# Cache pages in units of two pages of one cache, 8 KB on each partition

## The reference

```python
# 8 sequences, 16 pages of 128 tokens each, 8 stick-breaking and 8 forgetting heads of 128
gather = lambda cache: cache[page_table].reshape(B, past, *cache.shape[2:])
# stick breaking: A[t,s] = sigmoid(z_ts) * prod_{s<j<t} (1 - sigmoid(z_tj))
z = jnp.einsum('bqhd,bkhd->bhqk', q, k) * SCALE
later = lax.cumsum(log_stay, axis=3, reverse=True) - log_stay
a = jnp.exp(jax.nn.log_sigmoid(z) + later)
# forgetting: softmax with logit[t,s] += c[t] - c[s], c = cumsum(log f)
```

## Time and profile before

| | us |
|---|---|
| median of three runs | 1514.88 |
| the profiled execution | 1516.05 |
| its span, first to last instruction | 1514.3 |
| TensorE, VectorE busy | 1315.7, 673.4 |
| granted TensorE clock, mean | 0.939 |

### The profile page before, as it was taken

The page is one execution under the profiler, slowest core; times in us unless marked ns, Lnnn a source line. Parts: engine busy times, 40 slices in busy tenths (PEclk is TensorE's granted clock), DMA queues, the critical chain, the costliest instruction groups (busy, mean ns, idle before and its releaser), DMA issues. The chain is left out here.

```text
span 1514.3 us, 26133 instructions
## 1 busy us (share of the span) xinstructions
PE 1315.7 (87%) x8622; PEld 870.3 (57%) x8622; DVE 673.4 (44%) x4778; ACT 233.6 (15%) x453; POOL 75.4 (5%) x119
## 2 busy tenths in 40 slices
PE   7999788889789899856899987789999999999992
PEld 4678455566556566533667743466666565655561
DVE  4437855676676675677846466021000100000004
ACT  2111002112212212213011021101111010111011
POOL 1000000000000000001000001001100010001000
PEclk8899989899999999976999998979999999999997
DMA  9776999999999999999999989999999999999984
GB/s 302 248 260 229 385 397 391 396 383 381 382 377 390 383 379 392 387 405 398 351 403 402 401 320 390 399 414 379 422 428 428 427 424 423 422 419 414 416 341 178
DMA packets 170382, 570.39 MB, mean 377 GB/s; under 512 B 17401, under 2 KB 75562, under 8 KB 156954
## 3 DMA queue, kind: packets, MB, share of 16 engines
q1 hardware_dynamic: 145616, 541.70, 91.4%
q10 hardware_dynamic: 21762, 22.58, 4.3%
q0 software_dynamic: 2896, 4.86, 0.9%
HBM read 558.26 MB, written 15.67 MB: 379 GB/s over the span
## 5 line engine op out<-in xcount | busy, mean ns | idle before, releaser
L128 DVE CUSTOM_DVE_ANT_0 ws<-ws,xgT 128x128 f32<-128x128 f32 x1792 | 387.8, 284 | 204.7 <-DMA ws<-in_cache_fox_k 186.0
L979 PE MATMUL bank<-xn,ws 128*128 128x264 f32 x1152 | 289.9, 407 | 10.5 <-DMA ws<-in_w_in 10.5
L979 PEld LDWEIGHTS bank<-xn,ws 128*128 128x128 f32 x1152 | 223.0, 199 | 110.9 <-issue 54.8
L1912 PE MATMUL bank<-ws,xgT 128*64 128x256 f32 x1024 | 231.4, 386 | 16.7 <-DMA ws<-in_w_expert_up 12.1
L1914 PE MATMUL bank<-ws,xgT 128*64 128x256 f32 x1024 | 231.5, 386 | 0.0
L964 PE MATMUL bank<-ws,PR 128*32 128x512 f32 x1024 | 150.8, 668 | 78.3 <-DMA ws<-in_cache_fox_v 73.8
L1912 PEld LDWEIGHTS bank<-ws,xgT 128*64 128x64 f32 x1024 | 140.3, 139 | 104.6 <-issue 22.2
L128 DVE DVE_READ_ACCUMULATOR2_ANT Z<- 128x1 f32 x1792 | 141.8, 79 | 0.0
L1914 PEld LDWEIGHTS bank<-ws,xgT 128*64 128x64 f32 x1024 | 140.3, 139 | 0.0
L2113 DVE COPY gu<-bank 128x256 f32<-128x256 f32 x32 | 13.6, 425 | 269.4 <-PE bank L1914 269.4
L1084 PE MATMUL bank<-qo,ws 128*128 128x256 f32 x512 | 117.0, 387 | 6.2 <-DVE qo L1521 5.2
(11 more groups left out here) (433 smaller groups left out, 971.4 us busy)
## 6 DMA issues: line engine op xcount, KB each, us to landing
ws<-in_cache_sb_k SPq DMA_DIRECT2D x128, 512.0 KB, 9.1
ws<-in_cache_fox_k SPq DMA_DIRECT2D x128, 512.0 KB, 13.0
ws<-in_cache_sb_v SPq DMA_DIRECT2D x128, 512.0 KB, 9.2
ws<-in_cache_fox_v SPq DMA_DIRECT2D x128, 512.0 KB, 12.8
ws<-in_w_expert_gate SPq DMA_DIRECT2D x32, 2048.0 KB, 16.1
ws<-in_w_expert_up SPq DMA_DIRECT2D x32, 2048.0 KB, 20.0
ws<-in_w_expert_down SPq DMA_DIRECT2D x32, 2048.0 KB, 16.9
ws<-in_w_in SPq DMA_DIRECT2D x24, 2048.0 KB, 21.3
```

The source lines that it names most:

```text
L128: ins = dve.tensor_tensor_reduce(k, k, qb[:, (g * H + h) * HD:(g * H + h + 1) * HD], 1.0, 0.0, ALU.mult, ALU.add, Z[:, n % 2, g, h, t:t + 1])
L979: mm = pe.matmul(out[:, 0:T], w[:, c, m * P:(m + 1) * P], xn[:, c, :], start=(c == 0), stop=(c == KC - 1))
L1912: pe.matmul(bank[2 * k][0:SLOTS, 0:256], lhs, ws[:, wg, c * 256:(c + 1) * 256], start=(c == 0), stop=(c == KC - 1))
```

## The change

A slot now holds two pages of **one** cache: step p of a sequence serves cache p % 2 (even steps stick breaking, odd steps forgetting) and page pair G = p % 16 // 2. A page is read as 64 rows of 8 KB (two neighbouring tokens each). The first DMA of a unit writes the page that comes at 2G+1 in the table's order to the even partitions 0, 2, ... 126, the second writes the page at 2G to the odd ones. So partition 2r holds tokens 2r and 2r+1 of one page, and partition 2r+1 those of the other. The slots' bytes, their number and the number of DMAs stay: 512 DMAs of 512 KB for the pages, each now 64 partitions x 8 KB. Each DMA has a `value_load` of its own. Scoring a slot is still 16 instructions, the values of a slot still 4 matmuls.

```diff
+def load_unit(sp, ring, u, rows, ptr, p, n_phys, landed):
+    n, G = p // PAGES, p % PAGES // 2
+    for half in range(2):
+        t = n * PAGES + 2 * G + 1 - half
+        page = sp.value_load(ptr[0:1, t:t + 1], min_val=0, max_val=n_phys - 1)
+        sp.dma_start(ring[half:P:2, u, :], rows[p % 2][bass.ds(page, 1)].rearrange("a r f -> (a r) f")).then_inc(landed, 16)
 def load_key_page / load_value_page   (now load_key_unit / load_value_unit; waits as before)
-    page = sp.value_load(ptr[0:1, p:p + 1], min_val=0, max_val=n_phys - 1)
-    for k in range(2):
-        sp.dma_start(kring[:, u, k, :], caches[k][bass.ds(page, 1)].rearrange("a p f -> (a p) f")).then_inc(S[f"k{u}"], 16)
+    load_unit(sp, kring, p % 4, key_rows, ptr, p, n_phys, S[f"k{p % 4}"])
-        key_caches = [a[n][0].rearrange("n p h d -> n p (h d)") ...]
+        key_rows, value_rows = ([a[n][0].rearrange("n (r j) h d -> n r (j h d)", j=2) ...] ...)
```

The start's key halves become units of 1 MB (16 instead of 32) through two positions, later four:

```diff
-HALF_POS = [i % 4 for i in range(20)] + [0, 1, 4, 5, 6, 7, 2, 3, 0, 1, 4, 5]
+UNIT_POS = [i % 2 for i in range(10)] + [0, 2, 3, 1, 0, 2]
 (sync engine, with the q_chunk loads between them where they were)
-                for i in range(9):  key_half(i)      ... range(9, 15), range(15, 20), range(20, 22), range(22, 32)
+                for i in range(4):  key_unit(i)      ... range(4, 8),  range(8, 10),  10,            range(11, 16)
```

The token order inside a slot is no longer the partition order, so the sums over later tokens change. In the start, on TensorE and VectorE:

```diff
-                for half in range(2):
-                    pe.matmul(out[:, :], tri_gt[:, :], LFT[:, half * 512:(half + 1) * 512], ...)
-                    for k in range(4):
-                        mm = pe.matmul(out[:, k * P:(k + 1) * P], totb[:, half * 4 + k, :], later[:, :], ...)
+                for b in range(2):
+                    for half in range(2):                      # out: 64 partitions of bank[2 + b]
+                        for j in range(2):                     # 256 columns each
+                            pe.matmul(out...[:, :, j], tri_in[:, j, :], lft[:, :, 1 - half], ...)
+                        for k in range(4):                     # 128 columns each
+                            mm = pe.matmul(out[:, k * P:(k + 1) * P], totb[:, b * 4 + k, 0:64], later2..., ...)
+                (after head(0); VectorE has copied both banks to LFT)
+                for i in range(2):
+                    mm = pe.matmul(bank[2 + i][:, :], weave, LFT[:, i * 512:(i + 1) * 512], start=True, stop=True)
+                (VectorE) two copies of 128 x 512 more, tensor_reduce to odd_row, two tensor_scalar to tri_s
```

and for each of the 8 sequences:

```diff
-                own.step(dve.tensor_tensor(sp_h[:, :, 1:PAGES + 1], by_head(zr), by_head(zs), ALU.add))
+                own.step(dve.tensor_tensor(sp_a[:, :, :], by_head(zr), by_head(zs), ALU.add))
+                own.step(dve.tensor_tensor(sp_h[:, :, 1:GROUPS + 1], sp_a[:, :, 0:PAGES:2], sp_a[:, :, 1:PAGES:2], ALU.add))
-                pe.matmul(bank[CH][:, P:2 * P], tri_ge[:, :], sp_h[:, :, 1:PAGES + 1], ...)
-                pe.matmul(bank[CH][:, P:2 * P], ones[:, :], run[:, :, 0:PAGES], ...)
+                pe.matmul(bank[CH][:, P:2 * P], tri_s[:, :], pair_of(sp_h[:, :, 1:GROUPS + 1]), ...)
+                pe.matmul(bank[CH][:, P:2 * P], ones[:, :], pair_of(run[:, :, 0:GROUPS]), ...)
-                dve.scalar_tensor_tensor(out=ts, ...).then_inc(S["ts"], 1)
+                own.step(dve.scalar_tensor_tensor(out=ts, ...))
+                dve.tensor_tensor(odd_t, odd_t, sp_a[:, :, 0:PAGES:2], ALU.add).then_inc(S["ts"], 1)
```

More of the change, by code:

```diff
@@ L259, in hybrid_step @@
         zr = sb("zr", [P, H * PAGES], where=bctx)
-        sp_h = sb("sp_h", [P, H, PAGES + 1], where=bctx)
-        run = sb("run", [P, H, PAGES + 1], where=bctx)
+        sp_a = sb("sp_a", [P, H, PAGES], where=bctx)
+        sp_h = sb("sp_h", [P, H, GROUPS + 1], where=bctx)
+        run = sb("run", [P, H, GROUPS + 1], where=bctx)
+        tri_s = sb("tri_s", [P, P], where=bctx)
+        odd_row = sb("odd_row", [P, 1], where=bctx)
         ts = sb("ts", [P, H * PAGES], where=bctx)
         zx = sb("zx", [P, H * PAGES], where=bctx)
-        tri_gt, tri_le, later, grow = ts, zr, zx, zs[0:48, :]
+        tri_le, later, grow = zr, zx, zs[0:48, :]
+        tri_in = ts[:, :].rearrange("p (j r) -> p j r", j=2)
         lfr, LFT, totb = (blk[:, i * 1024:(i + 1) * 1024] for i in range(3))
         totb = totb.rearrange("p (h n) -> p h n", h=H)
+        weave = blk[:, 3072:3200]
         rstd = osum[:, 0:T]
@@ L300, in q_chunk, with key_unit @@
                     sp.dma_start(chunk(n), w_in[:, :, c0:c0 + 256]).then_inc(W[Q_SLOT[n]], 16)
-                def key_half(i):
-                    g, t, u = i // PAGES, i % PAGES, HALF_POS[i]
-                    before = [j for j in range(i) if HALF_POS[j] == u]
+                def key_unit(i):
+                    g, G, u = i // GROUPS, i % GROUPS, UNIT_POS[i]
+                    before = [j for j in range(i) if UNIT_POS[j] == u]
                     if before:
                         sp.wait_ge(A["hused"], before[-1] + 1)
-                    page = sp.value_load(ptr[0:1, t:t + 1], min_val=0, max_val=n_phys - 1)
-                    sp.dma_start(khalf[:, u, :], key_caches[g][bass.ds(page, 1)].rearrange("a p f -> (a p) f")).then_inc(A[f"kh{u}"], 16)
+                    load_unit(sp, kring, u, key_rows, ptr, 2 * G + g, n_phys, A[f"kh{u}"])
                 for t in (2, 0, 1):
@@ L664, in vector @@
                 own.step(dve.tensor_scalar(fr[:, :], fl[:, :], -1.0, 0.0, ALU.mult, ALU.max))
-                for i in range(5, 9):
-                    score_half(i)
+                for i in range(2, 4):
+                    score_first(i)
                 dve.wait_ge(A["fln"], 1)
@@ L669, in vector @@
                                          in1=fa[:, :], op0=ALU.mult, op1=ALU.subtract).then_inc(A["fgc"], 1)
-                for i in range(9, PAGES):
-                    score_half(i)
+                for i in range(4, GROUPS):
+                    score_first(i)
                 dve.wait_ge(A["fg"], FG["ct"])
@@ L692, in hybrid_step @@
                             gates, extra, many, iota, destc, drow, xs_pc, g_pc, sqs, srs, outs, start, A,
[L693 removed]
+                            osum, blk, PR, zs, zr, sp_a, sp_h, run, ts, zx)
         done_with(nc, A)
@@ L960, in values @@
                 pe.wait_ge(S[f"v{u}"], 32 * (s // 4 + 1))
-                for g in range(2):
+                for j in range(2):
                     for half in range(2):
-                        r0 = 32 * (2 * g + half)
-                        mm = pe.matmul(bank[0][r0:r0 + 32, :], PR[:, g, t, :],
-                                       vring[:, u, g, half * 512:(half + 1) * 512],
-                                       start=(t == 0), stop=(t == PAGES - 1))
+                        r0, c0 = 32 * (2 * g + half), j * H * HD + half * 512
+                        mm = pe.matmul(bank[0][r0:r0 + 32, :], PR[:, g, 2 * G + j, :], vring[:, u, c0:c0 + 512],
+                                       start=(G == 0 and j == 0), stop=(G == GROUPS - 1 and j == 1))
                 mm.then_inc(S["vused"], 1)
```

179 lines of the change are left out of this document (95 added, 84 removed).

## The result

The changed kernel takes 1541.02 us (median of 4 runs, 1532.53 to 1544.82) beside 1515.04 us for the kernel before (4 runs, 1513.42 to 1525.88): a ratio of 1.0145, with a 95% interval of 1.0116 to 1.0175. It is slower by about 22 us. 1498 us was forecast, a gain of 17 us. The profiled execution took 1544.82 us, with a span of 1543.0 us.

What follows compares the result with a forecast made beforehand. From about 152 us on, the kernel was taken as a queue of DMA bytes. 1516.05 - 25 (packets) + 2 (TensorE) + 6 (start) = 1499, so 1498 as median; own range 1479 to 1513, 8-in-10 range 1479 to 1820.

Steps and rivals of the forecast that it cites:

- small things: Extra VectorE operations, sums' stride-0 operands and a second page-number load per slot: all taken as nothing.
- The packets: Page loads while the DMA engines are full: 8 KB rows instead of 4 KB save 25 us (19 to 39).
- The 2 us given back to TensorE: At 720 to 900 us, TensorE busy 166.6 of 180 us: faster loads meet it, 2 us lost (0 to 8).
- Engines in each other's way: Page loads onto 64 alternate partitions: rival with pages at a lower rate despite full share, slower; chance 0.41.
- The straight line: Page packets: fixed cost of 13 ns per packet, 315 ns for 8 KB, giving the 25 us saving.
- The gain meets something else: Attention stretch: rival, TensorE bursts or sync issue bound two thirds, start costs 9 us, about 1516; 0.08 with another rival.
- The start: Before the steps: sums add 4.35 us and `weave` 1.98 to TensorE's path; 6 us taken (3 to 9).
- The sums: TensorE at the start: 4096 columns instead of 2048, 8.7 us instead of 4.35, so 4.35 us more.
- the 10 that the prediction named as its own refutation: At the start: a move of more than 10 us would show the prediction wrong.
- the sync engine's second page number: Slot issue in the steps: 1.57 to 2.3 us, hidden by queued loads, nothing; 35 us if uncovered.
- 8 KB stay whole: Page loads: 8 KB rows travel as 8 KB packets; the rival that they are cut to 4 KB had 2%.
- VectorE's new operations: Two more per sequence, 4 us beside DMA-bound time: cost nothing; 4 us if that cover went.

Runs made afterwards that it cites:

- E2: The kernel before, with both caches' values on two groups of 32 PSUM rows, loads as before: 1535.20 us, 1.0110.
- E9: E8 with its units loaded as 128 partitions x 4 KB, decoding outputs not the reference's: 1522.64 us, 1.0046 of the kernel before.
- E8: E6 and E7 together, 8 KB packets kept: 1510.44 us, 0.9946 of the kernel before.
- E7: E1 with the start's sync queue reordered, w_in blocks 6 and 7 ahead of units they stood behind: 1534.16 us, 1.0102 of the kernel before.
- E1: The changed kernel with a slot's four value matmuls on four PSUM row groups, by page and half: 1537.90 us, 1.0128 of the kernel before.
- E4: The changed kernel with one page-number load per unit, decoding outputs not the reference's: 1540.32 us, 1.0152 of the kernel before.
- E10: E8 with one page-number load per unit, decoding outputs not the reference's: 1511.71 us, 0.9957 of the kernel before.
- E5: E1 with units loaded as 128 partitions x 4 KB, decoding outputs not the reference's: 1524.86 us, 1.0048 of the kernel before.
- E6: E1 with the eight w_out blocks issued by the sync engine between page loads instead of by ScalarE: 1516.93 us, 0.9983 of the kernel before.
- E3: The changed kernel with units loaded as 128 partitions x 4 KB, decoding outputs not the reference's: 1537.67 us, 1.0124 of the kernel before.
- E12: The changed kernel with only the w_out blocks moved to the sync engine's queue, two row groups kept: 1531.39 us, 1.0091 of the kernel before.

## Why the prediction was wrong

**The step that failed is one that the sum does not have.** The part on small things counts new VectorE operations, sums and page-number loads, and passes over the values' matmuls, which stay four per step. It thereby costed them at nothing. Their number did stay (1024 records in both pages), but not what ran side by side: 1.06 us became 1.91 in the median step, 85 us more of TensorE by the page (128 x 0.85 would be 109, but 19 steps of before took 1.46 to 1.94 us, at a granted clock of 0.50 to 0.69). The row that warned stands in the earlier trace rows: TensorE was busy 267 of 300 us and 167 of 180, so 33 and 13 us of idle time were all that such a term could use. From 300 to 600 us it just fitted in (6 us left), in the output projection it did not, and E2 prices it alone at 16 us. The change reduced the four groups of PSUM partitions that a step's matmuls write to two.

**No queue beside the pages' was weighed.** The prediction costed the packets on q1 alone and did not ask who shares the engines with them. The earlier trace rows has the pages on SPq only; ScalarE's two loads of `w_out` and the store behind them were never read. This is the second step that failed. Longer packets on one queue took a share from the other, 143 to 97 GB/s, and a store in ScalarE's queue made it TensorE's wait of 19.7 us. This is 8 to 10 us of the loss as the kernel stands and 21 us once the first cause is gone.

**The packets, 25 us (19 to 39).** Mechanism right, term too large. Pages alone in the changed kernel, 253 to 261 us: 1.023 x 16 x 8 / 3.39 = 38.6 us of an engine per MB, where 38.5 was forecast and 40.1 stood before. The other windows with pages alone give the same 38.6 at 417 to 420 GB/s. The row of the changed kernel, and behind it one of E9, 4 KB in units, 215 to 223 us, 1.026 x 16 x 8 / 3.28 = 40.0:

```profile
q1 hardware_dynamic: 518, 3.39, 102.3%
```

```profile
q1 hardware_dynamic: 897, 3.28, 102.6%
```

At 38.6 the queue alone would have saved (40.1 - 38.6) x 251.7 / 16 = 24 us. The step from this to the time failed: it took every byte from 152 us to the end of the steps as bound by the queue. Where there was room it brought 12 to 15 us (E9 to E8), and in the changed kernel the steps from 0 to 72 took 5.8 us less than before. The 2 us given back to TensorE (0 to 8) were sized too small.

**Engines in each other's way** (0.41, 1806 us) did not happen: 38.6 us per MB at 424 GB/s with a full share. The straight line had 38.5 for the packet size alone, so at most 0.1 us per MB is left in this row for where the rows land. That what one engine writes slows another, from which the 1806 us and the upper end of the range, 1820, were worked out, no run shows; why the rows on 16 partitions moved at 104 GB/s was not tested. The result fell into the range only because the range reached up to this rival, and for none of its reasons. *The gain meets something else* (1516) came nearest in kind: TensorE did become the bound, but by time that the change added, not by work that it had.

**The start, 6 us (3 to 9).** It moved by 13.1 us, beyond the 10 that the prediction named as its own refutation. The sums were cheaper than forecast: the next head begins 1.35 us later (50.13 against 48.78) and not 4.35. They run from 43.98 to 50.13 us, 6.15 us and not the 8.7 forecast. One reason is in the earlier trace rows: the forecast priced a column by 4.35 us for 2048, and the first matmul there takes 1.77 us, the second of the same size 1.02:

```profile
46.93 1.02 PE L537 MATMUL bank<-blk,ts 128*128 128x512 f32 x2
```

The granted clock is 0.51 from 44.43 to 45.80 us there and 1.00 behind it; in the changed kernel it is 1.00 from 43.7 to 50.13 us. Two matmuls of 512 and eight of 128 columns at full clock would be 2 x 1.85 = 3.7 us (46.93 to 48.78, twice), so 4096 columns one after the other 7.4 us, an estimate; the 1.2 us less that were measured suggest that part of the matmuls with outputs of 64 partitions ran side by side (a record of L558 and one of L561 start at 45.66 and 45.70 us and last 0.39 and 0.27 us). `weave` took 1.88 us, 1.98 forecast. What was missed is the queue: units of 1 MB put the issue of w_in block 6 back by 9.3 us and the landing of block 7, for which TensorE then waits, by 7.2 us (3.8 at the issue, 3.4 behind it). The prediction said that behind the wait stood ten halves as five units; it did not follow the w_in blocks that stand between them. E7 gets back that wait and has a clock of 1.00 behind it, 4.9 us of its start against E1's. The last 1.7 us for VectorE and the slow L150 after it stay, in E7 too (3.36 and 5.11 us, the clock 0.65 from 157.6 to 162 us).

**The terms together**, an estimate: the packets brought 8 to 11 us less than the 23 (25 less 2 given back), the start cost 7 us more than the 6, and the two terms that the sum does not have cost 24. That is 39 to 42 us, beside a miss of 43 by the medians (1541 less 1498) and 39 by the ratio (22 + 17).

**Right as forecast:** the sync engine's second page number is hidden (E4, E10), though a slot's cycle is 2.49 us and not 2.3; 8 KB stay whole (414 of the 518 packets from 253 to 261 us, the other 104 are under 512 B); VectorE's new operations cost nothing visible (677.4 us against 673.4); the expert stretch has its 428 GB/s as before.

**What stays open.** E1 and E5 start at 171.6 and 165.6 us with a difference of rows only. In these single profiles E5 waits 0.7 us less for w_in (1.49 against 2.22) and 0.7 less for VectorE (2.37 against 3.04), and its L150 takes 3.60 us and not 5.29, at a clock of 1.00; but the start with 8 KB rows itself varies by 4 us from profile to profile (168.7 in E6, 172.8 in the changed kernel), and so does that with 4 KB rows (165.6 in E5, 169.8 in E3), so the share that hangs on the packets was not separated. E1's last stretch has a clock of 0.91 and 27 us without TensorE work (201 less 173.74); what the clock alone cost there was not measured.

## What to carry to other kernels

When a change regroups data, count not the instructions of the consumer but which of them ran side by side, by duration per step against a lone one's; a wait for a DMA may hide the loss until the DMA gets faster (here TensorE's waits for value pages fell from 73.8 to 15.1 us while its own work grew by 80.7). Before packets on one queue are made longer, look at what else the engines serve at that time: here two queues moved 716 and 715 packets in 15 us, and the one with 2 KB packets paid, 143 GB/s becoming 97. And where undoing a suspected cause wins nothing, add that cause alone to the kernel before, and undo it again together with the next suspect: E1 alone would have acquitted the row groups, which E2 and the pair of E12 and E6 show at 14 to 16 us.

## What the runs showed of the hardware that was not expected

- Four fp32 matmuls of 128 x 512 onto 32 columns each take 1.06 us on four groups of PSUM partitions (895.09 us, before), and 1.91 us on two groups (914.74 us, changed kernel), both at a clock of 1.00; one by itself, onto 128 columns, takes 0.99 us.
- Two hardware queues with work moved the same number of packets, 1063 and 1062 in 15 us before, 716 and 715 in the changed kernel: 2 KB packets got 143 GB/s beside a queue of mostly 4 KB packets and 97 beside one of mostly 8 KB packets.
- DMAs of 64 rows of 8 KB onto every second partition ran at a full share (1.023 from 253 to 261 us), 417 to 424 GB/s in windows of 8 us of pages alone, against 408 GB/s for 128 rows of 4 KB.
